# Block 1's last output projection in two passes over its weights, and the first products of block 2's layers moved ahead

## What is computed

```python
# block 1, end of each layer; then the next layer starts with x @ w_in[l]
out = merged @ w_out                                  # (512,1024) @ (1024,1024)
x = _layer_norm(DEEPNORM_ALPHA * x + out, ln_g, ln_b)
# block 2, start and end of each layer
h = _rmsnorm(x, norm_g[l])
z = jnp.einsum('bsd,de->bse', h, w_in[l])             # gate "Ag", query "Aq", ... are slices of w_in
...
x = x + jnp.einsum('bsm,md->bsd', mix, w_out[l])
```

## Time and profile before

| | |
|---|---|
| median of 3 runs | 1529.29 us (1528.23 to 1529.31) |
| profiled execution, own time | 1525.2 us |
| its span | 1523.4 us, TensorE's granted clock 0.978 on average |
| TensorE matmul busy | 1418.6 us, 93% of the span |
| VectorE / ScalarE / GpSimd busy | 846.7 (56%) / 720.5 (47%) / 372.9 us (24%) |
| chain that ended last | TensorE 74%, VectorE 12%, ScalarE 8%, DMA 2% |

### The profile page before, as it was taken

The page is one execution under the profiler, slowest core; times in us unless marked ns, Lnnn a source line. Parts: engine busy times, 40 slices in busy tenths (PEclk is TensorE's granted clock), DMA queues, the critical chain, the costliest instruction groups (busy, mean ns, idle before and its releaser), DMA issues.

```text
span 1523.4 us, 21528 instructions
## 1 busy us (share of the span) xinstructions
PE 1418.6 (93%) x8202; PEld 1101.0 (72%) x8202; DVE 846.7 (56%) x1545; ACT 720.5 (47%) x1541; POOL 372.9 (24%) x265
## 2 busy tenths in 40 slices
PE   7999999999999999999996889988997989988997
PEld 6767777778986777687796756665776856655776
DVE  4565436457643642546667464567556274457555
ACT  3555446555245553655533443445444344445443
POOL 2232122255221422224530111311112112311011
PEclk9999999999999999999998999999999999998999
DMA  6413451126243212112543323420314422411311
GB/s 224 111 30 90 114 126 46 49 75 234 88 138 68 69 56 84 42 47 63 181 120 103 69 69 70 90 71 21 111 50 112 96 69 52 94 61 44 98 63 56
DMA packets 191213, 131.57 MB, mean 86 GB/s; under 512 B 91526, under 2 KB 181254, under 8 KB 191110
## 3 DMA queue, kind: packets, MB, share of 16 engines
q1 hardware_dynamic: 187334, 116.02, 28.0%
q10 hardware_dynamic: 3776, 14.16, 2.4%
HBM read 117.84 MB, written 12.32 MB: 85 GB/s over the span
## 4 chain that ended last, share of the span: by engine, by line
PE 74%; DVE 12%; ACT 8%; issue 3%; DMA 2%; POOL 1%; SPq 1%; ACTq 0%; DVEq 0%; POOLq 0%
PE pb L1446 19%; PE pb L1448 17%; PE pb L1447 17%; PE pb L1529 6%; PE pb L1468 6%; PE pb L1507 4%; ACT prob L1585 2%; ACT tmp L1585 2%; ACT wh L1604 1%; DVE xl L1959 1%; DVE wl L1952 1%; PE pb L1491 1%; DVE prob L2204 1%; DMA wr<-w_out 1%; PE pb L1479 1%
## 5 line engine op out<-in xcount | busy, mean ns | idle before, releaser
L2345 POOL TENSOR_TENSOR wl<-wr,wh 128x512 fp32r<-128x512 f32 x170 | 242.8, 1428 | 879.7 <-ACT wh L1604 876.0
L1446 PE MATMUL pb<-xh,wl 128*128 128x512 f32 (+1 forms) x880 | 358.9, 408 | 26.5 <-DVE xl L1959 12.5
L1447 PE MATMUL pb<-xl,wh 128*128 128x512 f32 (+1 forms) x880 | 330.4, 376 | 0.0
L1448 PE MATMUL pb<-xh,wh 128*128 128x512 f32 (+1 forms) x880 | 330.4, 375 | 0.0
L1952 DVE TENSOR_TENSOR wl<-wr,wh 128x512 fp32r<-128x512 f32 x200 | 162.5, 814 | 180.2 <-ACT wh L1604 180.0
L1446 PEld LDWEIGHTS pb<-xh,wl 128*128 128x128 f32 x880 | 171.7, 195 | 99.2 <-issue 56.1
L1604 ACT CAST wh<-wr 128x512 fp32r<-128x512 f32 x370 | 210.4, 604 | 32.0 <-PE pb L1448 21.8
L1448 PEld LDWEIGHTS pb<-xh,wh 128*128 128x128 f32 x880 | 171.5, 195 | 29.8
L1447 PEld LDWEIGHTS pb<-xl,wh 128*128 128x128 f32 x880 | 172.4, 196 | 22.3 <-issue 3.6
L1585 ACT ACTIVATE prob<-prob,small 128x512 f32<-128x512 f32 (+3 forms) x128 | 76.3, 597 | 138.8 <-DVE small L2167 138.6
L1446 PE MATMUL pb<-wh,xl 128*128 128x256 f32 x448 | 130.8, 292 | 8.2 <-DVE xl L2110 3.3
(11 more groups left out here) (197 smaller groups left out, 2435.7 us busy)
## 6 DMA issues: line engine op xcount, KB each, us to landing
wr<-w_in SPq DMA_DIRECT2D x39, 1024.0 KB, 5.2
wr<-w_in SPq DMA_DIRECT2D x48, 256.0 KB, 4.6
wr<-w_out SPq DMA_DIRECT2D x10, 1024.0 KB, 5.2
wr<-w_branch SPq DMA_DIRECT2D x48, 128.0 KB, 2.3
x<-prob SPq DMA_DIRECT2D x12, 512.0 KB, 2.6
wr<-w_out SPq DMA_DIRECT2D x48, 128.0 KB, 3.0
wr<-w_mem_kv SPq DMA_DIRECT2D x4, 1024.0 KB, 5.5
prob<-x ACTq DMA_DIRECT2D x2, 2048.0 KB, 10.7
```

The costliest lines, as they stand in the source:

```text
L1446: e.matmul(ps, ll, rh, start=start, stop=False)
L1447: e.matmul(ps, lh, rl, start=False, stop=False)
L1448: t = e.matmul(ps, lh, rh, start=False, stop=stop)
L2345: t = e.tensor_tensor(wl[:, j % 2, c0:c1], wr[:, j % 2, c0:c1], wh[:, j % 2, c0:c1].bitcast(F32), ALU.subtract)
```

## The change

It has four parts. First, `wo` of the last layer of block 1 is listed twice (eight weights of 1 MB in place of four). Its first pass makes tiles 0 and 1 and its second pass tiles 2 and 3. The steps of `settle` for tiles 0 and 1 are emitted between the products of the second pass, and their transposes in its last weight. Second, a new function `first_pieces` makes the products of `Ag` and `Aq` with the first half of the tokens, with the steps of `settle` for the later tiles emitted between them; it is called at both starts of a layer of block 2. Third, at the boundary between block 2's layers, tiles 0 and 1 are turned before the last `part` products (tiles 2 and 3), not after them, and the casts that are due are emitted ahead of them. Fourth, at the end of block 1's first layer `resid` is emitted ahead of the steps of `settle` and no longer behind them.

```diff
-        out += [("wo", 8, 256, l, 256 * m) for m in range(4)]
+        out += [("wo", 8, 256, l, 256 * m) for _ in range(1 + l) for m in range(4)]
...
+    def first_pieces(ep, late):
+
+        two = [wnext("Ag"), wnext("Aq")]
+        st["hold"] = True
+        held = [[GR[0].take() for _ in range(2)] for _ in range(2)]
+        for w, h in zip(two, held):
+            advance_late(late)
+            halves(w, ep, 0, h)
+        while advance_late(late):
+            pass
+        return two, held
...
+        def out_product(w, m, i):
+            out_tile(m, i, drain(gemm("tok", w, 0, 256, ("m", l), range(8), tile=i)))
+
+        late = []
+        if l:
+            two = [wnext("wo") for _ in range(2)]
+            st["hold"] = True
+            held = {(m, i): drain(gemm("tok", two[m], 0, 256, ("m", l), range(6), tile=i, end=False, stop=False))
+                    for m in range(2) for i in range(2)}
+            for m, i in held:
+                out_tile(m, i, drain(gemm("tok", two[m], 0, 256, ("m", l), (6, 7), tile=i, b=held[m, i], start=False)))
+                if i:
+                    wdone(two[m])
+                    st["hold"] = False
+            for m in (2, 3):
+                w = wnext("wo")
+                for i in range(2):
+                    out_product(w, m, i)
+                wdone(w)
+            late += [settle(i) for i in range(2)]
+            for m in range(4):
+                w = wnext("wo")
+                for i in (2, 3):
+                    out_product(w, m, i)
+                    advance_late(late)
+                    if m == 3:
+                        run(features(2, i - 2))
+                wdone(w)
+            late += [settle(i) for i in (2, 3)]
+            first = first_pieces(2, late)
+            give(*X, *X0)
+            break
...
         for i in range(4):
             for m in (2, 3):
-                b = drain(gemm("tok", pair[m - 2], 0, 256, ("m", l), range(8), tile=i))
+                out_product(pair[m - 2], m, i)
                 advance_late(late)
-                out_tile(m, i, b)
...
-    def project(l, br, box):
+    def project(l, br, box, opening=((None, None), ((), ()))):
         ep = 2 + l
-        two, held = [None, None], [(), ()]
+        two, held = opening
         if br == "A":
-            two, held = [wnext(br + "g"), wnext(br + "q")], [[GR[0].take() for _ in range(2)] for _ in range(2)]
-            st["hold"] = True
-            for w, h in zip(two, held):
-                halves(w, ep, 0, h)
             last_features(ep)
             halves(two[0], ep, 1, held[0])
...
@@ -1113,23 +1143,24 @@
                 wdone(box["w"])
                 st["hold"] = False
+                while due:
+                    tick()
+                if l == 0:
+                    run(features(3, 0))
+                    run(features(3, 1))
             for m in range(2):
...
             late.append(settle(i))
-            advance_late(late)
-            tick()
+            if l or i < 3:
+                advance_late(late)
         wdone(first["w"])
         if l == 0:
-            run(features(3, 0))
-            while advance_late(late):
-                pass
-            run(features(3, 1))
-        else:
-            while advance_late(late):
-                pass
+            first = first_pieces(3, late)
+        while advance_late(late):
+            pass
```

More of the change, by code:

```diff
@@ L898, in plan @@
         for i in range(4):
-            out_tile(1, i, drain(gemm("tok", w, 0, 256, ("m", l), range(8), tile=i)))
+            out_product(w, 1, i)
         wdone(w)
-        if not l:
-            mem_features(1)
+        mem_features(1)
         pair = [wnext("wo") for _ in range(2)]
-        st["hold"], late = True, []
+        st["hold"] = True
         for i in range(4):
             for m in (2, 3):
-                b = drain(gemm("tok", pair[m - 2], 0, 256, ("m", l), range(8), tile=i))
+                out_product(pair[m - 2], m, i)
                 advance_late(late)
-                out_tile(m, i, b)
                 if i == 3:
@@ L918, in plan @@
         st["hold"] = False
-        if l:
-            for i in range(2):
-                advance_late(late)
-                run(features(2, i))
-            while advance_late(late):
-                pass
-            give(*X, *X0)
-        else:
-            parts = mem_parts(1)
-            for turned in ((0, 1), (2,), ()):
-                next(parts)
-                advance_late(late)
-                for i in turned:
-                    run(features(1, i, (X[i],)))
-            rest_of(parts)
-            while advance_late(late):
-                pass
-    def project(l, br, box):
+        parts = mem_parts(1)
+        for turned in ((0, 1), (2,), ()):
+            next(parts)
+            advance_late(late)
+            for i in turned:
+                run(features(1, i, (X[i],)))
+        rest_of(parts)
+        while advance_late(late):
+            pass
+    def project(l, br, box, opening=((None, None), ((), ()))):
         ep = 2 + l
-        two, held = [None, None], [(), ()]
+        two, held = opening
         if br == "A":
-            two, held = [wnext(br + "g"), wnext(br + "q")], [[GR[0].take() for _ in range(2)] for _ in range(2)]
-            st["hold"] = True
-            for w, h in zip(two, held):
-                halves(w, ep, 0, h)
             last_features(ep)
@@ L1044, in plan @@
         box, tail = {}, iter(())
-        run(project(l, "A", box))
+        run(project(l, "A", box, first))
         first = {}
```

## The result

The changed kernel takes 1513.64 us (median of 5 runs, 1512.14 to 1517.45). The kernel before, run beside it, takes 1528.23 us (5 runs, 1524.46 to 1529.31). The ratio is 0.9913, its 95% interval 0.9893 to 0.9934: by the ratio it is 13.3 us faster (the two medians are 14.6 apart), where the forecast had 12.6 (1516.7 us). It ran once more among the experiments: 0.9931 (0.9916 to 0.9945), which is 10.5 us. The profiled executions have spans of 1523.4 and 1512.5 us, 10.9 apart.

What follows compares the result with a forecast made beforehand. TensorE was taken to bound the kernel, so the gain lies in its gaps, with VectorE the bound in the second pass. Savings of 9.6 and 3.0 us sum to 12.6, from 1529.3 to 1516.7 us; range 1508 to 1522.

Steps and rivals of the forecast that it cites:

- The second boundary: Between block 2's layers: 22.7 us in place of 32.3, 9.6 us less; bounds 8.0 to 10.
- the 1.6 us of clock: Second boundary: 96 matmuls took 13.1 us against 11.55 at full clock; this 1.6 us was to go.
- The first boundary: End of block 1: 4.7 us less by steps, 3.0 less after the clock; bounds 9.4 less to 1 more.
- the term for the clock: First boundary, second pass: waits of 3.8 and 2.9 us bring one more clock fall, costing 1.7 us.
- GpSimd's share: Second pass: VectorE slowed beside GpSimd, remainders 1.43 us rather than 0.68, `norm_x` 1 up to 3.9 rather than 2.6.
- the rival: First boundary gives nothing: GpSimd's lock costs its full price, some 4 us beyond the charge, clock falls twice; chance 0.18.
- The sign that the forecast named: Second pass: waits ended by VectorE's `wl`, with VectorE busy over 90% there, would show the forecast right.
- The loads: Four more MB on SP's queue, covered up to a landing of 7.2 us; costed at nothing.
- VectorE keeps up: Second pass: waits of 3.8 and 2.9 shrink to about 1 each, 8 to 9 us gained there; 1511; chance 0.17.
- the first boundary gives nothing: Clock falls twice and GpSimd's lock costs its full price, so only 9.6 us remains; 1519.7; chance 0.18.
- the loads starve the pass: Second pass: landings of 13.3 us make three rounds 6.1 us late each, 18.3 in all; 1535.0; chance 0.05.
- the 8.06 us wait only moves: Second boundary: late casts of `Aq` or tile 3's norm keep 4 us of the wait; 1520.7; chance 0.10.

Runs made afterwards that it cites:

- experiment 2: The kernel before with only the edits at the boundary between block 2's layers; 1516.36 us, ratio 0.9937.
- experiment 3: The kernel before with only block 1's last output projection changed (two passes over `wo`, first products of `Ag` and `Aq` behind); 1523.11 us, ratio 0.9983.
- experiment 1: The changed kernel with the old order in block 1's first layer, `settle`'s step ahead of `resid` again; 1512.64 us, ratio 0.9916.
- experiment 11: The changed kernel itself timed again, nothing altered, in the session of experiment 9 and experiment 10; 1515.71 us, ratio 0.9931.
- experiment 5: The changed kernel with tiles 0 and 1 turned behind the last `part` products again at the second boundary; 1517.56 us, ratio 0.9955.
- experiment 9: The changed kernel with one VectorE norm step of tiles 0 and 1 left out in block 1's last layer; 1512.02 us, ratio 0.9911.
- experiment 10: The changed kernel with `wo` streamed once, norm steps between that pass's products, and the old order in block 1's first layer; 1502.58 us, ratio 0.9844.
- experiment 4: The changed kernel with tile 1's norm steps begun one product after tile 0's in the second pass; 1512.86 us, ratio 0.9912.
- experiment 6: The changed kernel with the second pass's four `wo` loads each cut into eight DMAs with rows of 128 bytes; 1519.12 us, ratio 0.9963.

## Why the prediction was right, and where it was not

**The second boundary** was forecast at 9.6 us less; it measured 9.8, and alone 9.8 as well (experiment 2). The order came as worked out. The changed kernel's timelines of DVE and ACT there:

```profile
1162.18 1.29 DVE L2173 SCALAR_TENSOR_TENSOR setB<-prob,stats,scr 128x1024 f32<-128x1024 f32 x1
1168.28 2.47 DVE L1990 TENSOR_TENSOR xl<-pb,xh 128x512 fp32r<-128x512 f32 x4
1180.18 1.28 DVE L2173 SCALAR_TENSOR_TENSOR setB<-prob,stats,scr 128x1024 f32<-128x1024 f32 x1
1167.32 2.04 ACT L1646 CAST xh<-pb 128x512 fp32r<-128x512 f32 x4
```

The transposes start at 1164.97, the turned tiles are copied by 1169.4, and their last remainder is done at 1170.75, 1.5 us ahead of `Ag`'s first product at 1172.3. Tile 3's norm is through at 1181.5, 2.4 us ahead of the end of the 96 products at 1183.9, which run at full clock [the window above]. From the transposes at 1164.97 to the second half at 1187.52 it takes 22.55 us, where 22.7 was worked out. Every term held, the 1.6 us of clock among them, and in nine more executions with this order the stage was 31.70 to 31.74.

**The first boundary** was forecast at 3.0 less. The pair of profiles shows 1.4, and alone the edit gave 2.6 (0.9 to 4.4, experiment 3). This stage isn't steady: five executions with the same order there took 77.68 (experiment 1), 79.25, 79.27 (experiment 3), 79.27 (experiment 11) and 80.56 (experiment 5), and two with the old one 80.64 and 81.83 (experiment 2). Its steps in the changed kernel, one by one: the wait for `wo` 2, 1.65 forecast, 1.91. From the first mark to the start of the second pass, 26.1 forecast (769.03 to 795.1), 26.2. The pass's waits, 0.6, 3.8, 2.9 and 1.5 forecast (8.8), came as 1.24, 3.44, 1.79 and 1.56 (8.0). VectorE's work in it, 27.8 forecast, 28.8. The rest, 16.1 forecast, 16.0. What failed is the term for the clock, "waits of 3.8 and 2.9 are long enough for one more such fall, 1.7 us": it fell twice in the pass in all five, and in four of them the pass took 37.0 and not 33.7 + 1.7. In experiment 1 the two falls were one stretch of 6.8 us, the wait behind it shrank to 0.61, and the pass took 35.4, as forecast. (37.0 less 8.0 of waits and 3.4 of clock is 25.6, where 24.9 of work was counted.) Experiment 9 shows the one half of the mechanism: less work for VectorE shortens the waits. The other half, that shorter waits keep the clock up, is only seen side by side: in experiment 10 no wait passes 1.5 us up to the transposes and the clock stays up to there, but it fell behind waits of 1.20 elsewhere (773.90 in the changed kernel, half clock from 774.0).

**GpSimd's share** was charged by the row. Rows of the changed kernel, timelines of DVE and POOL:

```profile
807.62 3.84 DVE L2161 SCALAR_TENSOR_TENSOR prob<-prob,stats,setA 128x1024 f32<-128x1024 f32 x2
811.38 1.76 DVE L1983 TENSOR_TENSOR wl<-wr,wh 128x512 fp32r<-128x512 f32 x1
828.34 1.42 DVE L1983 TENSOR_TENSOR wl<-wr,wh 128x512 fp32r<-128x512 f32 x1
808.23 2.16 POOL L2376 TENSOR_TENSOR wl<-wr,wh 128x512 fp32r<-128x512 f32 x1
810.46 2.14 POOL L2376 TENSOR_TENSOR wl<-wr,wh 128x512 fp32r<-128x512 f32 x1
827.91 1.29 POOL L2376 TENSOR_TENSOR wl<-wr,wh 128x512 fp32r<-128x512 f32 x1 [4.33 <-ACT wh L1635]
```

Two steps that take 1.27 each by themselves took 3.84, and a remainder of 0.68 took 1.76: 1.3 and 1.1 us more, where the forecast had 1.3 and 0.7. The ends of the rows tell why. GpSimd's remainders end at 812.60 and 829.20, VectorE's, begun before that, at 813.14 and 829.76: 0.55 us behind, whatever was left of GpSimd's when they began (29 remainders of 128x512 in this trace do so). GpSimd is held up in turn, 2.16 and 2.14 us for 1.29 alone. The Trainium skill (SBUF — State Buffer, Who interferes with whom) says that a VectorE instruction with two SBUF inputs contends with a GpSimd one that reads SBUF, over ports that it calls an exclusive lock. The trace agrees: what is left of the other's instruction is waited out in full.

What the rival had wrong is how much is left, and how often. VectorE was held up at four places in the pass: at the two norm steps (1.3 us more), at the remainders at 811.38 (1.1) and 828.34 (0.7), and at a small step at 822.41 that took 1.19 for 0.22 (1.0). That is 4.1 us, where eight at the full price would be over 11 (the forecast's "some 4 us beyond what I charge" is too low for that: 8 x 1.4 less the 5.0 that it had charged is 6.2). VectorE's total in the pass was 1.0 us above the forecast. The sign that the forecast named, VectorE busy over 90% of the pass, was wrong by its own sum (27.8 of 33.7 is 82%): it was 78%, and 89% around the longest waits. VectorE delays the pass in a few places, by the order of its steps there (experiment 4) as well as by their sum (experiment 9).

**The loads** were costed at nothing. In the changed kernel ScalarE waits 6.10 us for `wo` ahead of the pass, until 795.72, 4.4 us before the first product with it, and no cast in the pass waits for `wo`; they landed in 5.2 us (median of the four). `Ag`'s first half came later than worked out. ScalarE waited 4.82 us for it until 826.63, 26.5 us into the pass and not 23.5, and TensorE didn't feel it, since the first product with `Ag` is only due at 837, behind a turned tile. Experiment 6 shows that the cover is real and finite.

**The step that was missed**: "`resid` ahead of `settle` in layer 1: nothing, within 1 us both ways, since TensorE doesn't wait there". It costs 2.9 us (experiment 1). TensorE didn't wait there, since ScalarE's casts came in time: they began at 412.65 before, and at 417.40 with the edit. The sentence looked at the engine that doesn't wait and not at the queue behind the step that was moved.

The forecast's saving came out 0.7 us from the measured 13.3 (2.1 from the 10.5 of experiment 11) in part by luck: 9.8 + 1.4 - 2.9 = 8.3 us are shown by the stages, against 12.6 forecast for the same parts. What the ratios show beyond that, 5.0 and 2.2 us, isn't assigned to any step. It is of the size of the 3.6 us by which the untouched stretches were shorter in the profiled execution, where 54.4 us ran at half clock, against 70.2 before. Why the falls outside the touched stages become fewer wasn't tried.

**The rivals.** That VectorE keeps up is out, by the pass's waits. That the first boundary gives nothing came near: its two falls of the clock came, and the 1.4 of the profiled pair is nearer to nothing than to 3.0. It is out by experiment 3 (0.9 to 4.4), and its price of GpSimd's lock by the 4.1 us above. That the loads starve the pass took rows of 128 bytes to show even in part. That the 8.06 us wait only moves is out by experiment 2.

## What to carry to other kernels

When a step is moved ahead of or behind another, follow what it now waits for through each in-order queue to the engine that sets the time: one norm step set one product later held a root, then a cast, then TensorE, and cost 2.9 us in a layer that the change wasn't about. When one pass is split in two to get the first tiles' norm under the second pass's products, the work of streaming the weights again lands on the engines that do the norm. A kernel with the norm's steps between the products of the single pass, without that work, took 11.4 us less at this boundary, with shorter waits and a higher clock. Two engines that hold each other up on shared ports are best read by the ends of their rows: a step that is longer than usual and ends at a fixed distance behind the other engine's was waiting for it.

## What the runs showed of the hardware

The clock was the larger unknown. In the changed kernel the two falls in the pass are full stretches of 3.40 us at a granted 0.50, each begun at or just behind the end of a wait for a remainder, and while TensorE works each costs some 1.7 us. A wait isn't always followed by one, and its length alone doesn't decide it: behind the same wait of 1.20 us at the start of the first boundary the clock fell in the changed kernel (774.0) and not in experiment 10 (768.95), and behind the same wait of 1.91 us the clock fell in five of ten profiled executions and not in the others. The kernel before had 13.6 us of half clock, from 820.4 to 834.0, around its waits of 6.78 and 5.24. In experiment 10 there was none from 626 until 834.4, behind the waits of 1.47 and 0.81 ahead of the transposes. In the profiled executions the half clock takes 54 us in the changed kernel and 70 in the one before. One such stretch more or less is 1.7 us, so two or three of them are as large as the spread between single executions; that they make it wasn't tried.

VectorE's steps with two inputs in SBUF and GpSimd's remainders hold each other up in full. A remainder of VectorE that takes 0.68 us alone took 1.42 to 1.78 where it began early in a GpSimd remainder, and ended 0.55 us behind it; two norm steps of 1.27 took 3.84, and the two GpSimd remainders beside them 2.16 and 2.14 for 1.29. `resid`, with one input in PSUM, took its 0.42 beside them all the same (806.83, with GpSimd's remainder from 806.85 to 808.15). In experiment 10, with GpSimd idle from 801 to 813, the same norm steps took 1.28 us each.
